# Delta rule branch: order of blocks, convolutions and weight splits, the relay's two queues, the spread on two engines

## What is computed

```python
kb = k * beta
lower = jnp.where(strict, jnp.einsum('bhnid,bhnjd->bhnij', kb, k) * decay, 0.0)
rhs = jnp.concatenate([v * beta, kb * jnp.exp(gc)[..., None]], axis=-1)
sol = lax.linalg.triangular_solve(lower + jnp.eye(CHUNK, dtype=jnp.float32), rhs,
                                  left_side=True, lower=True, unit_diagonal=True)
u, w = sol[..., :dv], sol[..., dv:]
a_intra = jnp.where(incl, jnp.einsum('bhnid,bhnjd->bhnij', q, k) * decay, 0.0)

def step(s, xs):
    u_i, w_i, q_i, k_i, a_i, gl_i = xs
    v_new = u_i - jnp.einsum('bhik,bhkv->bhiv', w_i, s)
    o_i = jnp.einsum('bhik,bhkv->bhiv', q_i, s) + jnp.einsum('bhij,bhjv->bhiv', a_i, v_new)
    s = s * gl_i[..., None, None] + jnp.einsum('bhik,bhiv->bhkv', k_i, v_new)
    return s, o_i
```

## Time and profile before

| What | us |
|---|---|
| median of three runs | 2531.59 |
| the profiled execution, its own time | 2527.7 |
| its span, first to last instruction | 2526.1 |
| TensorE busy | 2368.8 |
| VectorE busy | 1390.6 |
| ScalarE busy | 967.8 |
| GpSimd busy | 307.7 |
| head 1: last products of the levels, start | 202.73 |
| head 2: the same | 272.43 |
| head 2: VectorE's step 3, start | 225.27 |
| head 2: VectorE's last step, end | 230.70 |

### The profile page before, as it was taken

How to read it: one execution, slowest core, us unless ns; L and a number is a source line. 1 busy time by engine, 2 the same in 40 slices (tenths; PEclk the granted TensorE clock), 3 DMA queues, 4 the chain that set the end, 5 groups by cost and what they waited for, 6 DMA issues and landing times.

```text
span 2526.1 us, 48968 instructions
## 1 busy us (share of the span) xinstructions
PE 2368.8 (94%) x19152; PEld 2262.6 (90%) x19152; DVE 1390.6 (55%) x2593; ACT 967.8 (38%) x1852; POOL 307.7 (12%) x382
## 2 busy tenths in 40 slices
PE   7888789999999999999998887899999999999998
PEld 5787779999999999989987776899999999999898
DVE  5677753677333434663566766537773344356644
ACT  4445432333234424452364445223332353255422
POOL 1222201000012101110012222100000110011000
PEclk9999989999999999999999999999999999999999
DMA  7110114111234333124221011131113332222122
GB/s 270 49 43 26 40 39 149 43 43 51 101 105 105 82 109 99 57 64 147 83 87 56 26 43 34 60 134 35 51 48 89 88 90 82 79 70 81 54 101 84
DMA packets 66589, 195.42 MB, mean 77 GB/s; under 512 B 19960, under 2 KB 20126, under 8 KB 66256
## 3 DMA queue, kind: packets, MB, share of 16 engines
q1 hardware_dynamic: 51232, 149.35, 17.6%
q0 software_dynamic: 15152, 43.24, 6.4%
HBM read 177.97 MB, written 8.39 MB: 74 GB/s over the span
## 4 chain that ended last, share of the span: by engine, by line
PE 71%; DVEq 5%; DVE 4%; issue 2%; ACT 1%; DMA 1%; SPq 1%; POOL 0%; POOLq 0%; ACTq 0%
PE proj L765 45%; PE mix L765 23%; DVEq L2200 5%; PE mix L768 3%; DVE area L2189 1%; DMA area<-area 1%; POOL stat L529 0%; ACT area L1590 0%; DVE w_lo L2189 0%; SPq L466 0%; SPq L470 0%; ACT merged L2132 0%; ACT w_hi L1590 0%; DVE h_lo L2189 0%; DVE y_lo L2189 0%
## 5 line engine op out<-in xcount | busy, mean ns | idle before, releaser
L765 PE MATMUL proj<-h_hi,w_hi 128*128 128x320 f32 x3072 | 741.5, 322 | 60.3 <-issue 34.2
L765 PE MATMUL proj<-h_lo,w_hi 128*128 128x320 f32 x3072 | 708.5, 311 | 0.0
L765 PE MATMUL proj<-h_hi,w_lo 128*128 128x320 f32 x3072 | 704.7, 311 | 0.0
L765 PEld LDWEIGHTS proj<-h_hi,w_hi 128*128 128x128 f32 x3072 | 512.0, 191 | 75.9 <-issue 65.1
L2189 DVE TENSOR_TENSOR w_lo<-raw,w_hi 128x1024 fp32r<-128x1024 f32 x232 | 285.6, 1231 | 472.4 <-ACT w_hi L1590 470.9
L765 PEld LDWEIGHTS proj<-h_lo,w_hi 128*128 128x128 f32 x3072 | 521.3, 190 | 0.0
L765 PEld LDWEIGHTS proj<-h_hi,w_lo 128*128 128x128 f32 x3072 | 518.4, 190 | 0.0
L1590 ACT ACTIVATE w_hi<-raw 128x1024 fp32r<-128x1024 f32 x232 | 245.9, 1060 | 553.3 <-PE proj L765 351.0
L765 PE MATMUL mix<-area 128*128 128x128 f32 (+8 forms) x4576 | 387.4, 261 | 22.0 <-DVE area L2422 12.3
L765 PEld LDWEIGHTS mix<-area 128*128 128x128 f32 (+5 forms) x4576 | 329.0, 157 | 63.7 <-issue 32.3
L1590 ACT ACTIVATE area<-mix 128x384 f32<-128x384 f32 (+6 forms) x414 | 168.5, 432 | 547.1 <-PE mix L765 422.0
(11 more groups left out here) (310 smaller groups left out, 2632.9 us busy)
## 6 DMA issues: line engine op xcount, KB each, us to landing
raw<-in_w_in SPq DMA_DIRECT2D x128, 512.0 KB, 3.5
raw<-in_w_mb SPq DMA_DIRECT2D x96, 512.0 KB, 3.5
raw<-in_w_mod POOLq DMA_DIRECT2D x32, 512.0 KB, 4.5
area<-in_bias POOLq DMA_DIRECT2D x64, 128.0 KB, 4.7
raw<-in_w_out SPq DMA_DIRECT2D x16, 512.0 KB, 3.5
out_x<-area SPq DMA_DIRECT2D x10, 512.0 KB, 2.6
merged<-in_w_mod SPq DMA_DIRECT2D x8, 512.0 KB, 11.1
area<-area POOLq DMA_DIRECT2D x64, 64.0 KB, 2.0
```

The source lines that it names most:

```text
L765: return T.matmul(out, l, r, start=start, stop=stop)
```

## The change

Seven edits, all in branch A:

1. `relay`: SP issues three of five transfers each way, GpSimd two (tiles 3 and 4), behind its third masking product and behind `Rv`.
2. GpSimd's first mask waits for the decays (count `4 h + 2` of `A_own`) instead of the normed keys; the third mask has no wait of its own.
3. `A_decays(h + 1)` stands ahead of state step 2 instead of behind it, `A_blocks(h + 1)` ahead of step 3 instead of behind it. TensorE's Gram unit 11 goes ahead of the state products of step 3.
4. Convolution 0 and the split of block 4 h + 6 stand ahead of `A_scaled` (in the last head `A_lower` does); the split of block 4 h + 7 stands between pivots 8 and 9; `A_lower` and the output squares stand between `A_inverse` and the spread.
5. The spread of X and Y for direction 0 stays on VectorE, that for direction 1 goes to ScalarE. TensorE waits for each half.
6. `A_levels`: 18 pieces ahead, 6 inside; `A_out(h - 1)` behind `A_mid_d`; ScalarE copies Q of the last level ahead of XT. The first head's front units stand one or two pieces earlier.
7. ScalarE takes convolution input 1 ahead of the weight block 4 h + 7; in the last head the gates go ahead of the blocks.

Where the instructions stand shows in the lists of each engine (line, operation, written<-read, size, count, and the semaphores waited for).

The diff, cut to its core (left out: the declarations, counts of `A_qn` and `A_own` that shift with the new events, the first head's front units, and the loop that takes two groups of units):

```diff
+        SP_TILES = 3
+
+        def blocks_in(eng, t, sig):
+            eng.dma_start(Z_t[8 * t:8 * t + 8, :], C16[:, t, :]).then_inc(sig.sem, sig.step)
+
+        def inverses_back(eng, t, sig):
+            eng.dma_start(X16[:, t, :, :], ZO_t[8 * t:8 * t + 8, :]).then_inc(sig.sem, sig.step)
...
                 def relay(h):
 
-                    sp.wait_ge(A_own.sem, A_own.at(layer, 3 * h + 2))
+                    sp.wait_ge(A_own.sem, A_own.at(layer, 4 * h + 3))
                     held(sp)
-                    for t in range(TILES):
-                        sp.dma_start(Z_t[8 * t:8 * t + 8, :], C16[:, t, :]).then_inc(A_relay.sem, A_relay.step)
-                    sp.wait_ge(A_own.sem, A_own.at(layer, 3 * h + 3))
+                    for t in range(SP_TILES):
+                        blocks_in(sp, t, A_relay)
+                    sp.wait_ge(A_own.sem, A_own.at(layer, 4 * h + 4))
                     held(sp)
-                    for t in range(TILES):
-                        sp.dma_start(X16[:, t, :, :], ZO_t[8 * t:8 * t + 8, :]).then_inc(A_relay.sem, A_relay.step)
+                    for t in range(SP_TILES):
+                        inverses_back(sp, t, A_relay)
...
-                    pool.wait_ge(A_kqn.sem, A_kqn.at(layer, h + 1))
+                    pool.wait_ge(A_own.sem, A_own.at(layer, 4 * h + 2))
                     held(pool)
                     pt(dec, decT, A_mask(strict))
                     held(pool)
                     P.drain()
                     pt(dec, dec, A_cols(1, h)).then_inc(A_dm.sem, A_dm.step)
-                    pool.wait_ge(A_own.sem, A_own.at(layer, 3 * h + 1))
-                    held(pool)
                     pt(decT, decT, A_mask(tri))
-                    pool.wait_ge(A_own.sem, A_own.at(layer, 3 * h + 2))
+                    pool.wait_ge(A_own.sem, A_own.at(layer, 4 * h + 3))
                     held(pool)
                     P.drain()
+                    for t in range(SP_TILES, TILES):
+                        blocks_in(pool, t, A_relay_pool)
                     pt(decT, decT, A_both(gram[:, :, 1, :])).then_inc(A_dm.sem, A_dm.step)
 
...
+                    pool.wait_ge(A_own.sem, A_own.at(layer, 4 * h + 4))
+                    held(pool)
+                    P.drain()
+                    for t in range(SP_TILES, TILES):
+                        inverses_back(pool, t, A_relay_pool)
                     if h:
...
                 def A_level_q(h):
 
                     pe.wait_ge(A_su.sem, A_su.at(layer, 5 * h))
-                    pe.wait_ge(A_x.sem, A_x.at(layer, 5 * h + 1))
                     for d in range(2):
+                        if d == 0:
+                            pe.wait_ge(A_x.sem, A_x.at(layer, 5 * h + 1))
+                        else:
+                            pe.wait_ge(A_qn.sem, A_qn.at(layer, 6 * h + 1))
                         for t in range(TILES):
...
                     A_level_q(h)
-                    fill(17, 18)
+                    fill(18, 19)
                     A_level_d(h)
+                    fill(19, 21)
+                    A_mid_q(h)
+                    fill(21, 22)
+                    A_mid_d(h)
                     if h:
                         pe.wait_ge(proj_taken.sem, proj_taken.at(layer, u0 + 2))
                         A_out(h - 1, psum_a[(u0 + 1) % 2])
-                    fill(18, 20)
-                    A_mid_q(h)
-                    fill(20, 21)
-                    A_mid_d(h)
-                    fill(21, 22)
+                    fill(22, 23)
                     A_last_q(h)
-                    fill(22, 23)
+                    fill(23, 24)
                     A_last_d(h)
-                    fill(23, 24)
                     pe.wait_ge(A_x.sem, A_x.at(layer, 5 * h + 5))
+                    pe.wait_ge(A_qn.sem, A_qn.at(layer, 6 * h + 6))
                     pe.wait_ge(A_rest.sem, A_rest.at(layer, h + 1))
...
 
                     part((), 0, 1)
                     last_part(22, 23)
-                    for n, (mid, after) in enumerate(((((0, 1), 1, 1), ((2, 3), 1, 2)), (((4,), 2, 2), ((5,), 2, 2)),
-                                                      (((), 2, 4), ((6, 7, 8), 4, 4)), (((9, 10), 4, 5), ((11,), 5, 6)),
-                                                      (((12,), 6, 7), ((13,), 7, 8)))):
+                    for n, (mids, after) in enumerate(((((((0, 1), 1, 1),), ((2, 3), 1, 2))), ((((4,), 2, 2),), ((5,), 2, 2)),
+                                                       ((((), 2, 4),), ((6, 7, 8), 4, 4)), ((((9, 10), 4, 5), ((11,), 5, 5)), ((), 5, 7)),
+                                                       ((((12,), 7, 7),), ((13,), 7, 8)))):
                         def between():
...
 
+                def A_spread(h):
+                    act.wait_ge(A_relay.sem, A_relay.at(layer, 6 * h + 6))
+                    act.wait_ge(A_relay_pool.sem, A_relay_pool.at(layer, 4 * h + 4))
+                    for m in range(4):
+                        last = A.activation(XY[:, 2:4, :, 16 * m:16 * m + 16], X16[:, :, 2:4, :].rearrange("p t s j -> p s t j"), ACT.Copy, scale=own_16[:, m:m + 1])
+                    last.then_inc(A_qn.sem, A_qn.step)
+
...
+                    act.wait_ge(A_q.sem, A_q.at(layer, 4 * h + 4))
+                    copy(Q_last, cols(1536, 64), -1.0).then_inc(A_qn.sem, A_qn.step)
                     act.wait_ge(A_x.sem, A_x.at(layer, 5 * h + 4))
                     for c in SIDES:
-                        copy(XT[c, :, :, c], Y[c])
-                    act.wait_ge(A_q.sem, A_q.at(layer, 4 * h + 4))
-                    copy(Q_last, cols(1536, 64), -1.0).then_inc(A_qn.sem, A_qn.step)
+                        last = copy(XT[c, :, :, c], Y[c])
...
                     for d in range(2):
                         A_keys(h, Rk, 5, d)
                     if more:
+                        A_take(h + 1, 1)
                         A_hi(4 * h + 7)
                     else:
+                        join_gate(0)
                         A_hi(18)
-                        join_gate(0)
                     act.wait_ge(A_sb.sem, A_sb.at(layer, 5 * h))
-                    A_keys(h, kd, 3, 0)
-                    if more:
-                        A_take(h + 1, 1)
-                    A_keys(h, kd, 3, 1)
+                    for d in range(2):
+                        A_keys(h, kd, 3, d)
                     if not more:
+                        join_gate(1)
                         A_hi(19)
-                        join_gate(1)
+                    A_spread(h)
...
+                    dve.wait_ge(A_relay.sem, A_relay.at(layer, 6 * h + 6))
+                    dve.wait_ge(A_relay_pool.sem, A_relay_pool.at(layer, 4 * h + 4))
                     for m in range(4):
-                        last = V.tensor_scalar(XY[:, :, :, 16 * m:16 * m + 16], X16.rearrange("p t s j -> p s t j"), own_16[:, m:m + 1], None, ALU.mult)
+                        last = V.tensor_scalar(XY[:, 0:2, :, 16 * m:16 * m + 16], X16[:, :, 0:2, :].rearrange("p t s j -> p s t j"), own_16[:, m:m + 1], None, ALU.mult)
                     last.then_inc(A_x.sem, A_x.step)
...
                     more = h < HEADS - 1
+                    if more:
+                        A_convolve(h + 1, 0)
+                        A_lo(4 * h + 6)
+                    else:
+                        A_lower(h)
                     A_scaled(h)
-                    A_pivots(1, 7)
-                    if more:
-                        A_lo(4 * h + 6)
-                    A_pivots(7, 15)
+                    A_pivots(1, 9)
+                    A_lo(4 * h + 7 if more else 18)
+                    A_pivots(9, 15)
                     A_inverse(h)
                     if more:
-                        A_convolve(h + 1, 0)
-                        A_lo(4 * h + 7)
-                    else:
-                        A_lo(18)
-                    A_lower(h)
-                    A_spread(h)
+                        A_lower(h)
                     if h:
                         A_out_squares(h - 1)
+                    A_spread(h)
                     if more:
...
                     for n in range(5):
+                        if n == 2 and more:
+                            A_decays(h + 1)
+                        if n == 3 and more:
+                            A_blocks(h + 1)
                         A_step(h, n)
```

43 lines of the change are left out of this document (22 added, 21 removed).

## The result

The changed kernel takes 2564.4 us (median of 4 runs, 2562.6 to 2566.0), the kernel before 2531.3 us. The ratio is 1.0133, 95% interval 1.0115 to 1.0150: 33 us slower. The profiled execution has a span of 2564.4 us. The forecast said slower by 8.6 us and reached up to 2548, so the direction held and the size did not.

What follows compares the result with a forecast made beforehand. VectorE's chain to the level products and the levels bound the kernel. Per layer head 0 +2.4, heads 1 and 2 +1.9 each, head 3 -1.9: +4.3 us, +8.6 for two layers, so 2540.2 us; range 2514 to 2548.

Steps and rivals of the forecast that it cites:

- What bounds the kernel: Branch A: VectorE's chain up to the level products and the levels' length set the time; the 4.70 us weight wait costs nothing.
- GpSimd and VectorE in each other's way: Shared port: VectorE stands until GpSimd's product is through, e.g. four products take 4.01 us instead of 1.98.
- Part 1: Scan, decays before step 2 and blocks before step 3: last state step ends at 233.9 instead of 230.7, 3.2 us lost.
- Part 2: Convolution and weight split ahead of the scaling: convolution held 2.3 us by GpSimd, scaling ends at 242.4, 5.3 us late.
- Part 3: Relay on two queues, spread on two engines: 1.3 us less from the queues, 1.9 us won in all, bounds 1.2 and 2.4.
- Part 4: Inside the levels, heads 1 and 2: middle products sooner; fast clock -2.3, slow clock -0.8, taken as -1.5 us.
- Head 3: Last head: 10.00 us gate wait goes, level products 0.7 us later, levels -2.6, sum -1.9 us.
- Rival 3: The relay doesn't get shorter, GpSimd's transfers landing last at the old 5.3 us: +11 us, 2551 us; chance 0.04.
- The two layers read alike: Both layers of the kernel: +4.3 us per layer, so +8.6 us for the two.

Runs made afterwards that it cites:

- e1_scan_old: Changed kernel with the scan's part undone (decays and block products behind their state steps, old masking waits, old place of Gram unit 11): 2553.7 us.
- e3_masks_later: Changed kernel with GpSimd's triangular mask product moved behind its block transfers and its right-hand side product behind its inverse transfers: 2544.8 us.
- third recombination: Changed kernel with old scan, second split and lower part behind the inverse, GpSimd's gram product behind its inverse transfers, right-hand side product in the levels: 2499.1 us.

## Why the prediction was right in direction and wrong in size

The forecast was +4.3 us a layer, and layer 0 lost 20.6. Of the 16.3 us between, 13.0 lie in the chain (2.6, 2.5, 2.7 and 5.3 us in heads 0 to 3) and 3.3 in the levels. The steps that failed are the time behind state step 3, GpSimd's right-hand side product in heads 0 and 3, the relay back, and the clock inside the levels. The direction was not luck: the late scan and GpSimd's holds, on which the forecast rested, give back 8 and 17 us when they are undone (e1_scan_old, e3_masks_later).

**What bounds the kernel**: right. The weight waits went and gained nothing; the chain and the levels set the time.

**GpSimd and VectorE in each other's way**: right, and larger than priced. All places named (block products 3.15, convolution step 3.09, head 0's block products 6.18 us) stood as said, and moving GpSimd's products alone gave 19.5 us back (17.3 by the ratios). The Trainium skill (SBUF — State Buffer, Who interferes with whom) names the instructions that need the shared pair, and the traces agree: a `tensor_scalar` took 6.62 us for 0.55, a step with two SBUF inputs 3.09 for 0.89. What was not priced: head 0's convolution stood under two products (6.72 us for one step), and in the last head the same product lay on the scaling, 3.91 us instead of 1.29. The forecast had written "no convolution" there and let the product drop out of the sum.

**Part 1, the scan**: mechanism right, size off. The last state step was to end 31.2 us behind the last level products and ended at 33.2 (28.0 before). The blocks ended 0.5 us late; the step that failed is "about 2.0 us" for TensorE, ScalarE, TensorE and VectorE behind state step 3, which took 3.3 us (244.12 to 247.44). Rows of other steps would have warned of it: in the kernel before, steps 2 and 3 begin 4.2 and 5.8 us behind the update of S that they need, TensorE's filling pieces included, and both waited for TensorE. In head 3 the blocks took 3.93 us, and the last step ended 35.0 us behind, not 31.

**Part 2, convolution and split**: the step by itself (convolution 4.7 us with the hold) was right. The scaling ended 41.4 us behind the last level products, forecast 39.7, and the difference is no more than the scan's 2.0.

**Part 3, relay and spread**: the first relay alone won 1.5 us, but was hidden already. The 1.3 us for the relay back is a term that failed. From SP's first issue to the spread it took 5.3 to 5.4 us before; in the changed kernel it takes 4.4 to 4.6 in layer 0 and 5.1 to 5.3 in layer 1, so 0.7 to 1.0 us and 0 to 0.2 are won. GpSimd issues some 1 us behind SP, and its transfers need 2.8 us from issue to landing, not the 2.0 taken from the earlier trace rows. What also failed is the silence about what stands behind the two issues on GpSimd, and about what stands ahead of ScalarE's half of the spread. Alone, this part costs 14.6 us.

**Part 4, the levels**: two errors that hid each other. With TensorE kept at work the levels of layer 0 are 11.7 us shorter than before, with 1.7 and 5.1 us in heads 0 and 3, where the level products had run at a low clock before (2.33 and 2.40 us) and now take 1.38; the forecast had taken 2.6 us a head at most and nothing in head 0. And in the changed kernel the low clock took 9.4 us of it back. The forecast saw the 8 us of idle time, and the row that shows its price, but chose -1.5, nearer to the fast end. The slow end, -0.8, would have been right to 0.8 us in heads 1 and 2.

**Head 3** is the largest miss (+6.0 for +0.7): the blocks' hold and the last state step, 7 us together where 3.1 stood, and the scaling's 2.6 us.

**Rival 3** (the relay doesn't get shorter), given 0.04 and 2551 us, comes nearest in time, and is half right: GpSimd's transfers back do come late, and in layer 1 little is won, but the first relay did get shorter, and the rival's 11 us are not what was lost. The rivals each undid one term; none let several holds lie on the same chain, which is what happened.

**"The two layers read alike"** held for the chain (17.6 us lost in heads 1 to 3 of layer 1, 17.9 in layer 0) but not for the levels, which got 6.1 us shorter there and 2.3 in layer 0. A further 6.2 us were lost ahead of layer 1's first level products. Why the relay back is slower in layer 1 was not followed.

## What to carry to other kernels

Before filling a wait, see whether it will still be there once the other parts of the change are in: here the late scan had already hidden the relay, and the filling became pure serial work. When two engines can hold each other, follow each product of the one through the new timetable of the other, and count DMA issues on the one as a shift of its products. And merging several short waits of TensorE into one long one right ahead of latency-bound products has a price of its own; it is better to keep filling work for that place.

## What the runs showed of the hardware

- A VectorE instruction on 128x641 elements with one tensor input took 0.55 us alone and up to 6.62 us beside two GpSimd products of 2.46 and 2.34 us with 1.2 us of DMA issues between them: it did not get in between the two.
- In the changed kernel, behind 8.21 us of idle time, 40 products of 64 columns took 2.40 us and the 80 behind them 2.86, at a granted clock of 0.75 over the 10 us from there. Where unused products had filled the wait but for 2.62 us, the 40 took 1.38 us and the 80 took 3.47, at 0.83; behind 2.74 us, in layer 1 of the same run, they took 2.40 and 3.50, at 0.68. With the wait filled but for less than 1 us they took 1.38 and 2.55, at 1.00.
- A short wait right ahead is not enough by itself. In the third recombination (head 3) the level products began behind 1.22 us of idle time, but 5.01 us had stood 3.5 us of work earlier: they took 2.40 us, at a granted clock of 0.80.
- Two transfers issued by GpSimd took 1.27 us of its time, beginning about 1 us behind SP's three (267.41 against 266.43). With the median of 2.8 us from issue to landing the second lands at about 270.9 (an estimate), and the spread began at 271.02. In this kernel and in the one with relay and spread alone, this relay took from 0.4 us more to 1.0 us less than with five issues of SP.
